# Ten rotating expert places in a two-block transformer kernel, with single buffers for gathered rows and scaled outputs

## What is computed

```
top_logit, top_idx = lax.top_k(sel_logits, TOP_K_IN_GROUP)
top_w = jax.nn.softmax(top_logit, axis=-1) * g_prob[:, None]
for gi in range(N_GROUPS):
    hid = (jax.nn.silu(jnp.einsum("td,edf->tef", t, expert_w_gate[gi]))
           * jnp.einsum("td,edf->tef", t, expert_w_up[gi]))
    hid = hid * combine[:, gi, :, None].astype(hid.dtype)
    y = y + jnp.einsum("tef,efd->td", hid, expert_w_down[gi])
```

## Time and profile before

| | us |
|---|---|
| median of three runs | 943.61 |
| lowest and highest | 940.68, 949.6 |
| the profiled execution, its own time | 943.65 |
| its span in the profile | 941.8 |
| TensorE busy, matmuls | 889.5 |
| VectorE, ScalarE, POOL busy | 367.2, 174.3, 92.3 |
| mean granted TensorE clock | 0.986 of full speed |

### The profile page before, as it was taken

How to read it: one execution, slowest core, us unless ns; L and a number is a source line. 1 busy time by engine, 2 the same in 40 slices (tenths; PEclk the granted TensorE clock), 3 DMA queues, 4 the chain that set the end, 5 groups by cost and what they waited for, 6 DMA issues and landing times.

```text
span 941.8 us, 11299 instructions
## 1 busy us (share of the span) xinstructions
PE 889.5 (94%) x4615; PEld 557.5 (59%) x4615; DVE 367.2 (39%) x834; ACT 174.3 (19%) x359; POOL 92.3 (10%) x91
## 2 busy tenths in 40 slices
PE   6999899999999998999999999999999996899985
PEld 3446756776667663688779898577455332343331
DVE  5746816433323339363475221662256111111014
ACT  3126512100000001222241221350111100000001
POOL 0045303301101100300000000000122000000000
PEclk9999999999999999999999999999999998999998
DMA  9997847544334553033352022202597999999993
GB/s 368 431 422 280 343 182 296 196 178 179 143 137 168 200 203 134 1 136 132 127 219 103 1 90 95 85 8 90 205 393 289 386 425 423 428 420 427 424 415 135
DMA packets 22617, 219.29 MB, mean 233 GB/s; under 512 B 3297, under 2 KB 3569, under 8 KB 8098
## 3 DMA queue, kind: packets, MB, share of 16 engines
q1 hardware_dynamic: 19186, 205.76, 54.6%
q0 software_dynamic: 3376, 12.76, 3.6%
HBM read 219.69 MB, written 2.10 MB: 235 GB/s over the span
## 4 chain that ended last, share of the span: by engine, by line
PE 82%; DVE 7%; DMA 7%; ACT 2%; issue 1%; SPq 0%; DVEq 0%; ACTq 0%
PE psum L2276 12%; PE psum L2298 9%; PE psum L508 8%; PE psum L1361 8%; PE psum L463 6%; DMA scr<-in_gates 4%; PE psum L2064 4%; PE psum L1415 3%; PE psum L755 3%; PE psum L1383 3%; PE psum L2257 3%; PE psum L2036 3%; PE psum L582 3%; DMA ring<-in_stream 2%; PE psum L2008 2%
## 5 line engine op out<-in xcount | busy, mean ns | idle before, releaser
L2276 PE MATMUL psum<-hT,ring 128*128 128x256 f32 x512 | 115.4, 379 | 1.1 <-issue 1.1
L2276 PEld LDWEIGHTS psum<-hT,ring 128*128 128x128 f32 x512 | 97.1, 190 | 26.7 <-issue 14.2
L1361 PE MATMUL psum<-ring,hT 128*32 128x512 f32 (+1 forms) x352 | 73.8, 617 | 13.7 <-DMA scr<-in_gates 11.0
L508 PE MATMUL psum<-hT,ring 128*128 128x272 f32 x320 | 74.2, 393 | 0.0
L508 PEld LDWEIGHTS psum<-hT,ring 128*128 128x128 f32 x320 | 60.6, 190 | 12.9 <-issue 0.5
L2298 PE MATMUL psum<-scr 128*128 128x512 f32 x128 | 59.5, 592 | 0.0
L2737 DVE TENSOR_TENSOR scr<-ring 128x512 f32<-128x512 f32 x16 | 11.1, 691 | 121.6 <-PE psum L2298 121.6
L463 PE MATMUL psum<-hT,ring 128*128 128x256 f32 x256 | 57.8, 382 | 0.0
L1361 PEld LDWEIGHTS psum<-ring,hT 128*32 128x32 f32 (+1 forms) x352 | 21.5, 125 | 58.0 <-issue 55.2
L2064 PE MATMUL psum<-ring,hT 128*128 128x512 f32 (+1 forms) x128 | 53.1, 574 | 2.4 <-ACT hT L2369 2.4
L1747 DVE TENSOR_TENSOR scr<-psum,scr 128x256 f32<-128x256 f32 x11 | 4.7, 424 | 127.4 <-ACT scr L1520 127.4
(11 more groups left out here) (526 smaller groups left out, 1234.2 us busy)
## 6 DMA issues: line engine op xcount, KB each, us to landing
ring<-in_stream SPq DMA_DIRECT2D x54, 2048.0 KB, 9.2
ring<-in_gates SPq DMA_DIRECT2D x17, 2048.0 KB, 18.2
scr<-in_gates SPq DMA_DIRECT2D x8, 2048.0 KB, 23.5
ring<-in_downs SPq DMA_DIRECT2D x12, 1024.0 KB, 17.8
scr<-in_downs SPq DMA_DIRECT2D x10, 1024.0 KB, 22.8
rowB<-in_rows POOLq DMA_DIRECT2D x6, 1024.0 KB, 9.9
scr<-in_stream SPq DMA_DIRECT2D x3, 2048.0 KB, 18.4
scr<-in_downs SPq DMA_DIRECT2D x8, 512.0 KB, 15.2
```

Of the source, the lines that this page charges most:

```text
L508: last = mm(psum[:, g % 4, 0:L2], w[:, k, m * P:(m + 1) * P], hT[:, k, :], start=(k == 0), stop=(k == KD - 1))
L1361: last = mm(psum[i * w:(i + 1) * w, 2, :], xg[p % 2][:, k, i * w:(i + 1) * w], weights[:, k, :], start=(k == 0), stop=(k == KD - 1))
L2276: last = mm(psum[:, f if f < 4 else 0, 0:NT], w[:, k, m * P:(m + 1) * P], hT[:, k, META:L2], start=(k == 0), stop=(k == KD - 1))
```

## The change

- Two more places for expert chunks, ten in all, each put together from parts of tiles that are no longer read: `rowB`, `gnB`, the constants and the arena (`in_parts`). A chunk in the ninth place is loaded by three transfers, in the tenth by four. SyncE waits for the fourth `mgd` before the first arena place and for `perm` and `affine` before the tenth.
- The places are taken in another order (`turns`): three of the ring, the three of the arena, the two others of the ring, the two new ones. `PIECED` are now chunks 10 and 11, both with run-time numbers.
- To free the room: `xr`, `yg`, `pg` and `hp` have one buffer each. Gain and shift of the last norm come as eight short rows (`gain_rows`) and are spread over the partitions by eight matmuls with an identity column behind groups 4 to 7 (`last_gains`), copied by ScalarE into `last_row`. `at_next` lies in `hT`. The warm-up matmuls read another constant.
- The order of the experts is found through TensorE: counts also along the partitions, 26-wide comparisons on VectorE in front of `flag`, two small products for order and ranks, and `perm` right behind `first`.
- The last two gates are loaded in halves, first halves first, and TensorE starts the last `gate_up` with the first four k blocks. In front of them the last wait has one set of warm-up matmuls less.
- The down weights of an expert lie half by half in memory, so that each of the last eight transfers has rows of 4 KB instead of two of 2 KB. The last group runs down half 0, scatter half 0, down half 1, scatter half 1.
- Some semaphores change their names.

The core of the diff, without the renamings and the branch for crowded experts, which this input does not take:

```diff
             rows(4, 0, S.in_row0)
-            rows(5, 1, S.in_row1)
+            pool.dma_start(gain_rows, IN["rows"][5].rearrange("a (b n) -> (a b) n", n=NT)).then_inc(S.in_row1, 16)
...
-            for n in range(2):
-                link(nc.gpsimd.memset(xr[n], 0.0))
+            link(nc.gpsimd.memset(xr[0], 0.0))
...
-        XR = 3
+        XR = 1
...
-        yg = [rowB[:, 0, n, :] for n in range(2)]
-        pg = [arena(4896 + 256 * n, 256) for n in range(2)]
-        hp = [arena(5408 + 256 * n, 256) for n in range(2)]
+        yg = rowB[:, 0, 0, :]
+        pg, hp = arena(4896, 256), arena(5152, 256)
         turned = [arena(5920 + 256 * n, 256) for n in range(2)]
...
         NP = len(GROUPS_E)
-        SLOTS = RING + 3
+        WHOLE = RING + 3
+        SLOTS = WHOLE + 2
         LATE = 6
-        extra_slot = [arena(6944 + CH * n, CH) for n in range(SLOTS - RING)]
+        GAINS_AT = (4, 5, 6, 7)
...
-            mm(psum[:, 5, 2 * NE:3 * NE], C("ones"), mem[:, 1, :], start=False, stop=True).then_inc(S.lg_mm, 1)
+            mm(psum[:, 5, 2 * NE:3 * NE], C("ones"), mem[:, 1, :], start=False, stop=True)
+            for t in range(T):
+                last = mm(psum[0:RANKED, 5, 3 * NE:3 * NE + 1], mem[:, t, FIXED:NE], C("ones", 0, 1),
+                          start=(t == 0), stop=(t == T - 1))
+            last.then_inc(S.lg_mm, 1)
             keep_warm(6, 2)
+            pe.wait_ge(S.cmb, 2)
+            number = C("num")[0:RANKED, 0:1]
+            mm(psum[0:1, 5, ORDER_AT:ORDER_AT + RANKED], number, at_rank, start=True, stop=True)
+            mm(psum[:, 5, RANKS_AT:RANKS_AT + RANKED], C("ones")[0:RANKED, :], rank_diag, start=True, stop=True)\
+                .then_inc(S.lg_mm, 1)
+
...
+            def last_gains(q):
+
+                pe.wait_ge(S.in_row1, 48)
+                if q:
+                    pe.wait_ge(S.gains_v, q)
+                for c in range(2):
+                    j = 2 * q + c
+                    last = mm(psum[:, 3, c * NT:(c + 1) * NT], C("ident")[0:8, j:j + 1].broadcast_to([8, P]), gain_rows,
+                              start=True, stop=True)
+                last.then_inc(S.gains, 1)
+
...
-                    landed_wait(pe, GATE[e])
-                    if len(group) == 4 and e != group[-1] and p > LATE:
+                    if GATE[e] != LAST_GATES[1]:
+                        landed_wait(pe, GATE[e])
+                    if len(group) == 4 and e != group[-1] and p > LATE and GATE[e] != LAST_GATES[0]:
                         keep_warm(2, 3)
...
+                    if p == NP - 1 and k == KD // 2:
+                        landed_wait(pe, LAST_GATES[1])
...
+                if p - 1 in GAINS_AT:
+                    pe.wait_ge(S.gains_v, GAINS_AT.index(p - 1) + 1)
...
+                if p == NP - 1:
+                    for half in range(2):
+                        down(p, (half,))
+                        last_scatter(half)
+                    continue
...
-            for half in range(2):
-                last_scatter(half)
+                if p in GAINS_AT:
+                    last_gains(GAINS_AT.index(p))
...
-            if p >= 2:
-                eng.wait_ge(S.sct, p - 1)
+            if p:
+                eng.wait_ge(S.sct, p)
...
+            v.scalar_tensor_tensor(key, psum[:, 5, 2 * NE + FIXED:3 * NE], 64.0, C("tier"), ALU.mult, ALU.add)
+            v.scalar_tensor_tensor(key_col, psum[0:RANKED, 5, 3 * NE:3 * NE + 1], 64.0, C("num")[0:RANKED, 1:2],
+                                   ALU.mult, ALU.add)
             link(places_prefix(v, C("code")))
+            v.tensor_scalar(above, key[0:RANKED, :], key_col, None, ALU.is_gt)
             v.tensor_reduce(many, over, AX, ALU.add)
             link(places_member(v))
+            v.tensor_reduce(rank_col, above, AX, ALU.add)
             v.tensor_scalar(many, many, BIG + 0.5, None, ALU.is_gt)
             link(places_sum(v))
+            v.tensor_scalar(at_rank, C("rank")[0:RANKED, :], rank_col, None, ALU.is_equal)
+            v.tensor_scalar(rank_diag, C("ident")[0:RANKED, 0:RANKED], rank_col, None, ALU.mult).then_inc(S.cmb, 1)
             link(v.scalar_tensor_tensor(crowd, cmx, CAP + 0.5, many, ALU.is_gt, ALU.max))
             v.tensor_copy(flag[:, :], crowd).then_inc(S.flag, 1)
             link(v.tensor_tensor(at128, C("iota", 0, P).unsqueeze(1).broadcast_to([P, 4, P]),
...
+            dve.wait_ge(S.lg_mm, 3)
+            v.tensor_copy(ranks, psum[:, 5, RANKS_AT:RANKS_AT + RANKED])
+            order = psum[0:1, 5, ORDER_AT:ORDER_AT + RANKED]
+            link(v.tensor_tensor(low[0:1, :], C("order")[0:1, :], order, ALU.subtract))
+            v.scalar_tensor_tensor(perm[0:1, :], low[0:1, :], crowd[0:1, :], order, ALU.mult, ALU.add).then_inc(S.perm, 1)
...
-                link(v.scalar_tensor_tensor(X[:, t, :], z[t], mv[:, t, 0:1], rowB[:, 1, 0, :],
-                                            ALU.subtract, ALU.mult))
+                dve.wait_ge(S.gains_v, 4)
+                for half in range(2):
+                    f = slice(half * 512, (half + 1) * 512)
+                    last = v.scalar_tensor_tensor(X[:, t, f], b_(4 + 2 * t + half), mv[:, t, 0:1], last_row[half],
+                                                  ALU.subtract, ALU.mult)
+                link(last)
...
         freed = sorted(range(RING), key=lambda i: holds[i])
+        turns = freed[:RING - 2] + list(range(RING, WHOLE)) + freed[RING - 2:] + [WHOLE, WHOLE + 1]
         for m in range(AT["end"] - AT["experts"]):
-            slot_of[AT["experts"] + m] = m % SLOTS if m % SLOTS >= RING else freed[m % SLOTS]
+            slot_of[AT["experts"] + m] = turns[m % SLOTS]
...
+        in_parts = [((rowB[:, 1, :, :].rearrange("p a b -> p (a b)"), 0, 4), (cst[:, 640:2176], 4, 7),
+                     (lay[:, 512:1024], 7, 8)),
+                    ((arena(2848, 2048), 0, 4), (rowB[:, 0, 1, :], 4, 6), (lay[:, 0:512], 6, 7), (cst[:, P:640], 7, 8))]
...
+            def last_gates():
+
+                numbers = [expert(gate_of[n]) for n in LAST_GATES]
+                for half in range(2):
+                    f = slice(half * (CH // 2), (half + 1) * (CH // 2))
+                    for n, number in zip(LAST_GATES, numbers):
+                        sp.dma_start(ring_at(n)[:, f], IN["gates"][bass.ds(number, 1), :, f])\
+                            .then_inc(landed[slots[LAST_GATES[half]]], 16)
 
...
+                if n == AT["experts"] + RING - 2:
+                    sp.wait_ge(S.mgd, 4)
+                if n == AT["experts"] + SLOTS - 1:
+                    sp.wait_ge(S.perm, 1)
+                    sp.wait_ge(S.affine, 4)
                 if n < FIXED_END:
-                    sp.dma_start(ring_at(n), IN["stream"][n]).then_inc(landed[slots[n]], 16)
+                    for words, a, b in parts(n):
+                        sp.dma_start(words, IN["stream"][n][:, a * 512:b * 512]).then_inc(landed[slots[n]], 16)
                 elif n in LAST_DOWN:
...
-                    sp.dma_start(ring_at(n), IN["gates"][bass.ds(expert(gate_of[n]), 1)]).then_inc(landed[slots[n]], 16)
+                    g = expert(gate_of[n])
+                    for words, a, b in parts(n):
+                        sp.dma_start(words, IN["gates"][bass.ds(g, 1), :, a * 512:b * 512]).then_inc(landed[slots[n]], 16)
...
-        w = wd[e].reshape(2, P, DM).transpose(1, 0, 2)
+        w = wd[e].reshape(2, P, 2, 512).transpose(1, 2, 0, 3)
```

More of the change, by code:

```diff
@@ L1242, in build @@
         crowd, many = arena(908, 1), arena(909, 1)
-        ranks, low, rise, order, key, over = (arena(408 + RANKED * n, RANKED) for n in range(6))
-        above = scr[:, 5408:5408 + RANKED * RANKED].rearrange("p (a b) -> p a b", a=RANKED)
+        ranks, low, rise, key, over = (arena(408 + RANKED * n, RANKED) for n in range(5))
+        above, at_rank, rank_diag = (scr[0:RANKED, 5408 + RANKED * n:5408 + RANKED * (n + 1)] for n in range(3))
+        key_col, rank_col = scr[0:RANKED, 5488:5489], scr[0:RANKED, 5489:5490]
+        ORDER_AT, RANKS_AT = 3 * NE + 32, 4 * NE + 32
         perm = sb("perm", [P, RANKED], I32)
@@ L1395, in last_scatter, with down @@
                     mm(b_(4 + 2 * t + half), scat[p % 2][:, t * P:(t + 1) * P],
-                       yg[p % 2][:, half * 512:(half + 1) * 512], start=False, stop=True).then_inc(S.sct, 1)
-            def down(p):
+                       yg[:, half * 512:(half + 1) * 512], start=False, stop=True).then_inc(S.sct, 1)
+            def down(p, halves=(0, 1)):
                 group = GROUPS_E[p]
@@ L1407, in down @@
                     pe.wait_ge(S.xgv, 2 * (p + 2))
-                for half in range(2):
+                for half in halves:
                     if p == NP - 1:
@@ L1434, in pe_gathered @@
                     scatter(p)
[L1435 to L1436 removed]
+                if p in GAINS_AT:
+                    last_gains(GAINS_AT.index(p))
         def pe_dense(pe, mm):
[L1440 removed]
+            pe.wait_ge(S.cmb, 4)
             for t in range(T):
```

(15 more changed lines are left out.)

159 lines of the change are left out of this document (82 added, 77 removed).

## The result

| | before | after |
|---|---|---|
| median, us (9 runs each) | 941.54 | 935.82 |
| lowest and highest | 940.34, 949.6 | 933.35, 937.56 |
| profiled execution: its own time, span | 943.65, 941.8 | 933.47, 931.7 |
| mean granted TensorE clock | 0.986 | 0.992 |

The ratio is 0.9927, with a 95% interval of 0.991 to 0.9945: a gain of 0.73%, some 6.9 us. That is inside the forecast range (the measured time is 935.8, the forecast 933.4, between 929.5 and 938.5), but two thirds of the 10.3 us of the sum. By the border of 1% that the forecast set, it is "no change", the side that had 0.32. A part of the hit is the base: the kernel before now has a median of 941.54, where the forecast started from 943.65. From there the measured gain gives 936.8, still in the range but outside the 930 to 936.5 that had 0.62.

A forecast was written before the change was run, and what follows sets the result against it. The expert weight stream, at its DMA limit from 765 us after standing still twice, was taken as the bound; -9.97 + 0.3 - 0.5 + 0.5 - 0.9 + 0.3 = -10.3 from 943.65 gave 933.4 us, range 929.5 to 938.5.

The forecast's parts named there:

- The places, -9.97: Expert weight stream: two more places make every later landing two chunks earlier, 2 x 4.99 us, if TensorE keeps up.
- The single row buffer, nothing but 0.5 of stall: Expert groups: gathers still land before their turning, with 2.2 us to spare; only group 1 stalls TensorE, 0.5 us.
- The parts of the new places, +0.5: Six later gates land in pieces, 2.36 MB of them in 2 KB rows: 6.1 instead of 5.6 us.
- The forecast's rival, 1.4 us for each: Weight transfers: each piece pays its own start, 17 pieces x 1.4 = 24 us, giving 957 us; chance 0.04.
- The order earlier, +0.3: Before the first gather: added small operations start TensorE's first group about 1.2 us later; stream pays +0.3, bounds -0.3 and +1.2.
- Rows of 4 KB in the last downs, -0.5: Last down weights: 4 KB instead of 2 KB rows save between 0 and 1.0 us, 0.5 taken.
- The far rival: Last weight transfers: 4 KB rows also end the one-by-one running out of DMA engines; 928 to 930 us, chance 0.10.
- The end of the work, -0.9 + 0.3: Tail: scatter half 0 ahead of the last down gains 0.9 us; splitting two 1024-wide operations into four costs at most 0.3.
- TensorE level with the stream (rival, 0.13): Expert groups: TensorE falls behind by 3 to 7 us, giving 936 to 940 us; chance 0.13.
- The holes not filled (rival, 0.05): Stream before 716 us: late `perm` or late room for chunks 3 to 5 loses one chunk's worth; 938.4 us, chance 0.05.

The follow-up runs named there:

- the old turns: The changed kernel with ten places, but the five ring places taken first and the three arena places behind them, as before the change: ratio 0.9965 to the kernel before.
- The thirty: The changed kernel with ten more chunks of gates each loaded in four transfers instead of one, same bytes: ratio 0.9958 to the kernel before.
- the anchor run: The changed kernel again, no edit, timed beside its variants: 936.53 against 943.17 us for the kernel before, ratio 0.9933.

## Why the prediction was right or wrong, by its steps

**The places, -9.97: right.** Eight, nine and ten places land their last piece 5.2 and 5.0 us apart, where the sum had 4.99 for each. By the times the two are worth 8.5 us (1.0023 to 0.9933). Both figures already hold what ten places bring with them, 15 more transfers, or 1.2 us by the price below: 9.97 less 1.2 is 8.8, near the 8.5. That the landings say 10.2 is mostly the profiled execution of the eight places, 1.1 us slower than the median of its kernel. Chunk 21 landed at 783.8, forecast 786.7; the last gate at 906.7, forecast 906.3; the last piece at 916.8, forecast 916.9; the span is 931.7, forecast 931.5. This agreement is partly luck. The profiled execution was 2.0 us early at 643 us, and its first group started at 709.97 where 713.2 was forecast. Counted from k0 the stream gained 7.9 and 8.2 us on the two profiles of before, where the forecast, from 713.2 to 916.9, was 203.7 after k0: 3.1 us less than the 206.8 that it took. An error of 3.1 us in the stream was hidden by a k0 that came 3.2 us early.

**The single row buffer, nothing but 0.5 of stall: wrong, and by the landings the largest miss.** The step asked only whether a gather would be late for its turning. It wasn't: in the changed kernel's profile the gathers landed 5.6 to 10.4 us after their issue (5.0 to 11.3 in the earlier trace rows). The step didn't ask where the bytes of the gathers go. Three buffers let them run ahead into the holes, one keeps 0.63 MB of them in the full stream: 1.7 us in the landings, 0.9 by the times, which alone would not tell it from nothing. The stall in group 1, forecast at 0.5, was 0.07 us; it was 1.9 in the profile with the old turns, where the stream was full at that point.

**The parts of the new places, +0.5: sized by the wrong thing.** The step counted bytes in short rows. A transfer more costs 0.08 us in the full stream, so the 17 come to 1.0 to 1.4 us, as five of them (those of chunks 18 and 19) go out just ahead of 765. The forecast's rival, 1.4 us for each (2.1 less 0.62 is nearer 1.5), is too high by a factor of 17. The Trainium skill ("DMA: Bandwidth & Descriptors", Anatomy of one DMA) gives a transfer that GpSimd issues about 2.0 us of fixed time, most of it at its completion; added up over 30 more that would be an estimated 60 us, and the runs disagree with 2.4 where the queue, here SyncE's, is full. The thirty had rows of 8, 4, 2 and 2 KB, so the 0.08 us holds both the start of a transfer and its shorter rows, and no run parts them.

**The order earlier, +0.3: right at full clock, with a second price that wasn't in the sum.** From the router's first product to k0 it is 24.73 and 24.40 us before, and 24.81 in the changed kernel's profile. The added operations themselves took 0.8 us more between `mem` and the gather of group 0 (4.97 against 4.19 and 4.09), near the 1.0 to 1.2 of the step. But in seven of the twelve profiles of the changed kernel and its variants, a stretch of half clock fell on TensorE's gather of group 0. From the gather's start to k0 it then took 7.3 to 7.5 us instead of 5.42, and from the router to k0 26.9. Windows of the profile after (columns as in the earlier trace rows) and of the anchor run, at the same place:

```profile
700.00:706.00 6.00, 4.97 (x33) 3.47 (x33) 3.81 (x23) 0.00 (x0) 0.00 (x0) 1.00 0.08 31
706.00:711.00 5.00, 5.00 (x44) 4.42 (x44) 2.60 (x8) 1.87 (x2) 0.00 (x0) 1.00 0.77 262
```

```profile
700.00:706.00 6.00, 5.21 (x24) 3.04 (x25) 4.17 (x27) 0.27 (x2) 0.00 (x0) 0.77 0.19 78
706.00:711.00 5.00, 5.00 (x29) 5.00 (x29) 1.32 (x2) 0.00 (x0) 0.00 (x0) 0.59 0.56 175
```

A granted clock of 0.59 and 0.77 here is the level of 1.2 GHz for part of the window. It costs 2.1 us, in 7 of 12 on average 1.2. Whether the change brings it isn't settled: both profiles of before have such a stretch close by (0.94 from 680 to 711), one of them with 6.11 us from the gather to k0. A kernel with the new operations but without them in the chain wasn't run.

**Rows of 4 KB in the last downs, -0.5: within the bounds, as far as can be told.** The runs gave 1.0 us by the times (not told from nothing), 0.4 by chunk 43 to the last landing. The far rival, that longer rows end the slope of the last 11 us, falls: 285 GB/s from 906 to 917, where 269 stood before from 916 to 927.

**The end of the work, -0.9 + 0.3: half of it came.** The tail is 14.87 us, forecast 14.6, before 15.2: 0.3 gained instead of 0.6. The prediction said that of what the halves of the last gates free nothing shows. With whole gates and the scatters last, the kernel with ten places is 2.4 us slower. That doesn't refute the sentence, as that kernel also lacked the third set of warm-ups and its last gates ran at a clock of 0.75. At full clock its down would have started an estimated 0.9 us ahead of the last landing (918.6 against 919.5), where before it started 1.5 ahead (925.11, with the last landing at 926.57). What the runs do show is that the first halves give TensorE work ahead of the last landing, and that its gates then ran at a clock of 1.00 with one set of warm-ups less. The sum didn't price that. A kernel with whole gates and three sets of warm-ups wasn't run.

**TensorE level with the stream (rival, 0.13): the race was real, the rival not.** TensorE was busy 137 of 141 us and met its last gates within 0.04 us. But at least 13.6 us of that are warm-ups (130.58 against 117.00 busy from 765 to 900), which could all go without any effect. What the sum called a lead of 0.5 to 1 us had a cushion that it didn't count. With nine places TensorE was late by 1.2 us at the last gates, as shown there, so the rival was near.

**The holes not filled (rival, 0.05): did not happen.** `perm` came in time and the three arena places found their room. Its price, one chunk, was too high for the hole before 716, which left empty costs 1.5 us by the times and 2.5 by the landing. For the other, 672 to 680, the old turns cost 3.0 us by the times and 5.0 by the landing, which is the one chunk.

**The sum again**, against the ratio: -9.97 for the places, +1.0 to 1.4 for transfers, +0.9 to 1.7 for the gathers, +0.1 to 1.6 for the start (its upper end with the 1.2 of the clock), -0.4 to -1.0 for the rows of 4 KB, -0.3 for the tail, gives -9.3 to -6.0. The times say -6.9, with an interval from -8.5 to -5.2. The bounds are wide, so the sum agrees with the times without proving each term.

Still open: by these terms, with 0.2 for the halves of its last gates, the kernel with eight places and three row buffers should stand between 1.0 us faster and 1.1 slower than the kernel before, and it measured 1.3 us slower (1.0014, with an interval from 0.9997 to 1.003). The kernel before measured against itself on the same chip gave 1.0013, so the times don't tell the two apart. The landing does a little: k0 + 215.3 is 0.3 to 0.6 us later than in the kernel before, although the last down weights have rows of 4 KB. No run isolates why.

## What to carry to other kernels

When a stream of weights is the bound, its places are worth what the distance of release says, and that can be read from two landings in the trace before anything is built. But list everything else that shares the DMA engines: a buffer that is given up doesn't have to be late to cost, it is enough that its transfers move from idle time into the full stream. And when an experiment undoes a step, check what else goes with it: the whole gates came back here without one set of warm-ups that had stood ahead of them, and their price can't be read.

## What the runs showed of the hardware

- In a full stream, cutting a transfer costs 0.08 us for each piece more (30 pieces, 2.4 us), while a lone 256 KB transfer took 2.1 us.
- Transfers of 32 partitions with rows of 16 KB drop the stream from 420 to 255 GB/s although the DMA engines show as full (share 1.02): 40 transfers of 512 KB cost 95 us. The same bytes as transfers over 128 partitions with rows of 2 to 8 KB cost 2.4 us. The ten chunks are 21 MB, 50 us at 420 GB/s; if all of the 95 us are theirs they took 145, at an estimated 145 GB/s. The Trainium skill ("DMA: Bandwidth & Descriptors", The descriptor swizzle) maps partitions 0 to 31, like any such quarter, to 8 of the 16 ports into SBUF, by which one would estimate half the rate, 210 GB/s. The direction agrees with the run, the size doesn't; no run here shows the ports.
- The last set of gates ran at a granted clock of 0.75 (9.59 us) where TensorE had stood idle for 6.2 us before it, and at 1.00 (7.12 us) in both profiles of the kernel before, where warm-ups had left 2.0 us.
- Two profiles of the same program differ in k0 by 3.2 us (709.97 and 713.2 for the changed kernel), 2.1 of it by whether a short stretch of the lower clock falls on one gather. A difference of a few us between two single profiles has to be counted from a common event.
